# The order of VectorE's and GpSimd's work in the steps of a mixture-of-experts loop

## What is computed

```python
def routed_experts(xf, idx, wts, wg, wu, wd):
    ...
    padded = (counts + MOE_BLOCK - 1) // MOE_BLOCK * MOE_BLOCK
    ...
    def step(acc, inp):
        tok, w, e = inp
        xb = xf[tok]
        hid = jax.nn.silu(jnp.einsum('nrd,ndf->nrf', xb, wg[e].astype(F32))) * jnp.einsum('nrd,ndf->nrf', xb, wu[e].astype(F32))
        yb = jnp.einsum('nrf,nfd->nrd', hid, wd[e].astype(F32)) * w[..., None]
        acc = acc.at[tok.reshape(-1)].add(yb.reshape(-1, D_MODEL))
        return acc, None
```

## Time and profile before

| | us |
|---|---|
| median of three executions | 2057.08 |
| the profiled execution | 2054.86 |
| its span, first to last instruction | 2053.1 |
| TensorE busy in the span | 1992.9 (97%) |
| VectorE busy | 1134.7 (55%) |
| GpSimd busy | 781.3 (38%) |
| ScalarE busy | 505.2 (25%) |

### The profile page before, as it was taken

The page is one execution under the profiler, slowest core; times in us unless marked ns, Lnnn a source line. Parts: engine busy times, 40 slices in busy tenths (PEclk is TensorE's granted clock), DMA queues, the critical chain, the costliest instruction groups (busy, mean ns, idle before and its releaser), DMA issues.

```text
span 2053.1 us, 23779 instructions
## 1 busy us (share of the span) xinstructions
PE 1992.9 (97%) x7241; PEld 1005.4 (49%) x7242; DVE 1134.7 (55%) x3064; ACT 505.2 (25%) x1103; POOL 781.3 (38%) x717
## 2 busy tenths in 40 slices
PE   8999999999999999999999999999999999999994
PEld 6444667575544444444445554444444444444441
DVE  6221546776622222344776757966666666666645
ACT  3111554452312222224331221111111111111114
POOL 1762005622122221215990002654555545454531
PEclk9999999999999999999999999999999999999997
DMA  5421000011132222135257014999999999999964
GB/s 148 125 96 41 21 21 21 22 47 47 41 129 77 77 82 75 49 114 175 96 201 285 31 42 151 361 362 361 354 363 355 369 350 355 350 341 355 339 216 172
DMA packets 129639, 370.45 MB, mean 180 GB/s; under 512 B 33712, under 2 KB 65668, under 8 KB 103832
## 3 DMA queue, kind: packets, MB, share of 16 engines
q1 hardware_dynamic: 103960, 314.83, 41.3%
q0 software_dynamic: 23520, 54.61, 10.5%
q10 hardware_dynamic: 2080, 0.01, 0.1%
HBM read 320.57 MB, written 68.17 MB: 189 GB/s over the span
## 4 chain that ended last, share of the span: by engine, by line
PE 25%; DMA 20%; issue 4%; POOL 3%; DVE 3%; POOLq 0%; ACT 0%; SPq 0%; DVEq 0%
DMA sums<-arena,row_to 19%; PE banks L3219 9%; PE banks L2300 4%; PE banks L3235 4%; PE banks L2347 2%; POOL arena L2136 2%; PE banks L2014 2%; PE banks L279 1%; PE banks L2364 1%; PE banks L2323 1%; DVE arena L3212 1%; DVE index L3182 1%; DMA arena<-in_w_router_dram 0%; DVE arena L3337 0%; PE banks L3227 0%
## 5 line engine op out<-in xcount | busy, mean ns | idle before, releaser
L3219 PE MATMUL banks<-arena 128*128 128x512 f32 x1056 | 467.7, 596 | 3.9 <-issue 3.2
L3198 POOL DMA_INDIRECT arena<-h_rows,index x268 | 282.5, 1054 | 133.4 <-issue 78.8
L3219 PEld LDWEIGHTS banks<-arena 128*128 128x128 f32 x1056 | 197.4, 192 | 228.4 <-issue 228.4
L1720 PE MATMUL banks<-arena 128*128 128x512 f32 x672 | 299.0, 594 | 1.0 <-ACT arena L323 1.0
L3235 PE MATMUL banks<-arena 128*128 128x512 f32 x528 | 237.6, 593 | 1.3 <-ACT arena L3033 0.8
L3206 POOL DMA_INDIRECT sums<-arena,row_to x66 | 109.0, 1652 | 268.4 <-DMA sums<-arena,row_to 229.0
L279 PE MATMUL banks<-arena 128*128 128x512 f32 x416 | 192.1, 599 | 2.2 <-PEq L108 2.2
L1720 PEld LDWEIGHTS banks<-arena 128*128 128x128 f32 x672 | 123.1, 190 | 135.5 <-issue 133.9
L3212 DVE STREAM_TRANSPOSE arena<-arena 128x1024 f32<-128x1024 f32 x66 | 133.7, 2026 | 57.6 <-PE banks L3219 57.5
L3182 DVE TENSOR_SCALAR index<-row 32x1 uint32<-32x1 f32 x1072 | 155.2, 145 | 17.1
L3235 PEld LDWEIGHTS banks<-arena 128*128 128x128 f32 x528 | 100.1, 190 | 126.5 <-issue 124.8
(11 more groups left out here) (414 smaller groups left out, 2424.0 us busy)
## 6 DMA issues: line engine op xcount, KB each, us to landing
arena<-in_w_exp_gate_dram SPq DMA_DIRECT2D x66, 1024.0 KB, 7.1
arena<-in_w_exp_up_dram SPq DMA_DIRECT2D x66, 1024.0 KB, 10.6
arena<-in_w_exp_down_dram SPq DMA_DIRECT2D x66, 1024.0 KB, 16.4
arena<-in_w_in_dram SPq DMA_DIRECT2D x26, 1024.0 KB, 5.3
gates<-arena SPq DMA_DIRECT2D x60, 256.0 KB, 2.0
arena<-gates SPq DMA_DIRECT2D x15, 1024.0 KB, 7.6
arena<-h_rows,index POOLq DMA_INDIRECT x268
arena<-in_x_dram SPq DMA_DIRECT2D x8, 512.0 KB, 5.8
```

What stands on the lines that cost most here:

```text
L1720: mm = pe.matmul(gate_bank(n, b), left[:, k, :], right[:, k, :], start=(alone and k == 0), stop=(k == 3), skip_group_check=True)
L3198: return pool.indirect_dma_start(w.x[k][:, 256 * q:256 * (q + 1)], None, rows, bass.IndirectOffsetOnAxis(ap=g.index[:, k, q:q + 1], axis=0 ...
L3219: mm = pe.matmul(g.bank[:, 2, :].rearrange("p (a f) -> p a f", a=2), xT[:, k, :], wgu[:, :, k, :], start=(k == 0), stop=(k == KT - 1))
```

## The change

It moves work within a step and adds or removes no computation.

- VectorE's order in every step but step 0 is: take_rows(b-1), the reading of the list of b+3 (`take_list`), turned(b+1), select(b+4), hidden(b), result(b-1), and last the rest of index(b+3) (`make_index`). Of the two branches behind `if not has(i, c, -1)` the first is always taken.
- GpSimd issues scatter(b-1) first and gather(b+3) after it.
- `overflow_tables` has seven parts instead of four, done in steps 0 to 6. The four large operations are cut into halves of 24x64 elements a partition.
- `run` writes out steps 0 to 7; the hardware loop begins at step 8.

```diff
--- before.py
+++ after.py
@@ -2646,24 +2646,36 @@
 
     ovhot = g.region(TABLES, 48, NE)
     over, ovend, ones, iota48 = g.over, g.ovend, g.ones64, g.iota48
+    halves = slice(0, 24), slice(24, 48)
+
+    def reached(h):
+        then(dve.tensor_tensor(ovhot[:, h], bcast(iota48[:, h].unsqueeze(2), [P, 24, NE]),
+                               bcast(ovend.unsqueeze(1), [P, 24, NE]), ALU.is_ge))
+
+    def weighed(h):
+        then(dve.tensor_tensor(ovhot[:, h], ovhot[:, h], bcast(over.unsqueeze(1), [P, 24, NE]), ALU.mult))
+
     if part == 0:
         then(dve.tensor_tensor_scan(ovend, ones, over, 0.0, ALU.mult, ALU.add))
         then(dve.tensor_scalar(g.ovmore[:, 0:1], ovend[:, NE - 1:NE], -float(AHEAD), 1.0, ALU.add, ALU.max))
         then(dve.tensor_copy(g.ovn[:], g.ovmore[:, 0:1]))
-
-        then(dve.tensor_tensor(ovhot, bcast(iota48.unsqueeze(2), [P, 48, NE]),
-                               bcast(ovend.unsqueeze(1), [P, 48, NE]), ALU.is_ge))
+        reached(halves[0])
     if part == 1:
-        then(dve.tensor_reduce(g.ovef, ovhot, AX.X, ALU.add))
+        reached(halves[1])
+        then(dve.tensor_reduce(g.ovef[:, halves[0]], ovhot[:, halves[0]], AX.X, ALU.add))
+    if part == 2:
+        then(dve.tensor_reduce(g.ovef[:, halves[1]], ovhot[:, halves[1]], AX.X, ALU.add))
         then(dve.tensor_scalar(g.ovef, g.ovef, float(NE - 1), None, ALU.min))
         then(dve.tensor_copy(g.ovexp[:], g.ovef))
-    if part == 2:
-
+    if part == 3:
         then(dve.tensor_scalar(g.idle, ovhot[:, :, NE - 1], 2.0 * T, None, ALU.mult))
-        then(dve.tensor_tensor(ovhot, ovhot, bcast(over.unsqueeze(1), [P, 48, NE]), ALU.mult))
-    if part == 3:
-        then(dve.tensor_reduce(g.shift[:], ovhot, AX.X, ALU.add))
-
+        weighed(halves[0])
+    if part == 4:
+        weighed(halves[1])
+    if part == 5:
+        then(dve.tensor_reduce(g.shift[:, halves[0]], ovhot[:, halves[0]], AX.X, ALU.add))
+    if part == 6:
+        then(dve.tensor_reduce(g.shift[:, halves[1]], ovhot[:, halves[1]], AX.X, ALU.add))
         then(dve.tensor_tensor(g.shift[:], iota48, g.shift[:], ALU.subtract))
         then(dve.tensor_scalar(g.shift[:], g.shift[:], 1.0, float(P), ALU.add, ALU.mult))
         dve.tensor_tensor(g.shift[:], g.shift[:], g.idle, ALU.add).then_inc(tabled, 1)
@@ -2739,9 +2751,9 @@
     def run(eng, before, step, ready, after):
 
         before()
-        for c in range(4):
-            step(0, c)
-        with eng.Fori(1, NE // 4 - 1) as i:
+        for b in range(8):
+            step(*divmod(b, 4))
+        with eng.Fori(2, NE // 4 - 1) as i:
             for c in range(4):
                 step(i, c)
         ready()
@@ -2899,11 +2911,17 @@
                 else:
                     select_rows(g, dve, w, g.iota[:], b).then_inc(s["q"], 1)
 
-            def index(i, c):
+            def take_list(i, c):
                 dve.wait_ge(s["lst"], val(i, c) + 1)
                 if has(i, c, -4):
                     dve.wait_ge(s["to"], 2 * val(i, c) - 6)
                 list_rows(g, dve, w, c % 4).then_inc(s["list"], 1)
+
+            def index(i, c):
+                take_list(i, c)
+                make_index(i, c)
+
+            def make_index(i, c):
                 dve.wait_ge(s["list"], val(i, c) + 1)
                 index_flags(g, dve, w, c % 4).then_inc(s["flag"], 1)
                 dve.wait_ge(s["flag"], val(i, c) + 1)
@@ -2959,6 +2977,18 @@
                     hidden(i, c)
                     index(i, c + 3)
                     select(i, c + 4)
+                elif has(i, c, -1):
+                    take_rows(i, c - 1)
+                    if has(i, c, 3):
+                        take_list(i, c + 3)
+                    if has(i, c, 1):
+                        turned(i, c + 1)
+                    if has(i, c, 4):
+                        select(i, c + 4)
+                    hidden(i, c)
+                    result(i, c - 1)
+                    if has(i, c, 3):
+                        make_index(i, c + 3)
                 else:
                     take_rows(i, c - 1)
                     if has(i, c, 3):
@@ -2968,13 +2998,12 @@
                     if has(i, c, 1):
                         turned(i, c + 1)
                     hidden(i, c)
-                if has(i, c, -1):
                     result(i, c - 1)
-                else:
+                if not has(i, c, -1):
                     first.last_sum()
-                if isinstance(i, int) and i == 0:
                     dve.wait_ge(g.sums_begun, 64)
-                    overflow_tables(g, dve, c, then, s["tabled"])
+                if isinstance(i, int) and i < 2 and val(i, c) < 7:
+                    overflow_tables(g, dve, val(i, c), then, s["tabled"])
 
             def ready():
                 picked.extend(chosen_expert(dve, k) for k in range(AHEAD + 1))
@@ -3099,10 +3128,10 @@
                 first.gpsimd(pool, lambda b: gather(0, b))
 
             def step(i, c):
+                if has(i, c, -1):
+                    scatter(i, c - 1)
                 if has(i, c, 3):
                     gather(i, c + 3)
-                if has(i, c, -1):
-                    scatter(i, c - 1)
 
             def after():
                 pool.wait_ge(stored[0], 16 * (NE // 2))
```

## The result

The change costs 2%: 2100.64 us (median of four) against 2056.76 (2055.85 to 2059.7) on the same chip, a ratio of 1.0205, 95% interval 1.0193 to 1.0217. The profiled execution took 2099.67 us, its span 2097.8, that is 44.7 more than the span before. Lines of the changed kernel: up products L3248, lists L2830, turn of hidden L3256, down L3264; on VectorE turned L3241, select L3189, product of hidden L2946, result L2953; GpSimd's scatter L3235, gathers L3227.

A forecast was written before the change was run, and what follows sets the result against it. It took TensorE to bound the first half of the expert loop and the chain of scatters the second. Span 2053.1 less 1.7, plus 1.8 and 2.2 from span to median, gave 2055.4 us, range 2050 to 2067.

The forecast's parts named there:

- The lists of b+4 need select too, but select ends before H does, so that costs nothing more: TensorE's list products at the step's end: waiting for select adds nothing, as select ends before the product of hidden.
- The floor of 10.99: TensorE's step with select between turn and product of hidden: 10.99 us with the short restart, 11.36 at the loop boundary.
- The ring: Scatter, later gathers, turn, products and next scatter: 41.6 us for four steps, 10.4 a step, some 3 us in hand.
- L = 11.2: Length in us assumed for one link of the scatter chain, each scatter waiting for the last; 11.29 was the mean before.
- links over 11.5 fall where issues meet select: Scatter chain: reason given for taking 11.2 us a link, since select now has a fixed place away from the scatter.
- is covered: VectorE's index work behind the result: hidden in 4 us of idle time a step, ahead of the next turn.
- The start: Start of the expert loop: third expert's up products at 1291.1 instead of 1294.91, fourth scatter at 1327.9 instead of 1333.02.
- The end: Last experts: up products of the last at 1984.0, last scatter at 2014.4, 1.7 us less than before.
- Rival (b): Select on the path costs the long restart in every step, 11.36 us: 2069; chance 0.30 with long scatter links.
- Rival (a): Expert loop falls to TensorE's new floor, 10.99 us in every step, scatter links under 11.1: 2051; chance 0.27.
- rival (c): Full DMA engines decide, order does nothing in the loop, only the start counts: 2053 to 2060; 0.43 with the main forecast.
- The rule on the shared port: VectorE and GpSimd lock a port pair: select would hold each step's last gather 0.8 us, without changing the sum.

The follow-up runs named there:

- e9: Changed kernel with list products in the hardware loop reading expert 0's values at a fixed address and gathers ahead of the scatter again: 2063.21 us, ratio 1.0028.
- e1: Changed kernel with select ahead of the turn again, GpSimd's new order kept: 2075.06 us, ratio 1.0085.
- e3: Changed kernel with list products in the hardware loop reading expert 0's values at a fixed address: 2069.11 us, ratio 1.0056.
- e5: Kernel before with only GpSimd's order changed, scatter ahead of the gathers: 2074.89 us, ratio 1.0070.
- e13: Changed kernel with eight tiny products at the same register addresses ahead of TensorE's wait for select, in the hardware loop: 2070.33 us, ratio 1.0064.
- e6: Changed kernel with select ahead of the turn and gathers ahead of the scatter again, index work still last: 2063.11 us, ratio 1.0024.
- e7: Kernel before with only the tables in seven pieces and eight steps written out: 2058.34 us, ratio 1.0005.
- e14: Changed kernel with the eight tiny address-making products ahead of the wait and gathers ahead of the scatter again: 2064.53 us, ratio 1.0034.
- e2: Changed kernel with only GpSimd's order undone, gathers ahead of the scatter again: 2098.16 us, ratio 1.0199.

## Why the prediction was wrong

It said 2055.4 us, 2050 to 2067; 2100.64 was measured, 31.6 us above the slowest case that it priced (2069). By its own steps:

- **"The lists of b+4 need select too, but select ends before H does, so that costs nothing more"** is the step that failed, and it is worth 0.7 to 0.8 us in each of 51 steps, some 40 us. It took the duration of the lists, 0.34 us, from a place where their wait had long been met. I had looked at when the wait is met and not at what TensorE does between the wait and the products. In the trace of before nothing comes to register-addressed products through a wait, but the size stood there all the same: the eight address instructions of its list line start between 1530.1 and 1531.0, hidden under other products (the view of L2818 above). Behind the wait they alone take these 0.9 us, and the lists with them 1.05, for the 0.34 that the forecast took.
- **The floor of 10.99** was right: product of hidden at +10.20 for 10.21, written-out steps of 11.01, and a median of 11.01 for the steps of e9 that aren't at the loop boundary. At the boundary six of e9's twelve steps are 11.33 to 11.38, for a forecast 11.36; the others are longer, up to 12.25.
- **The ring** was mis-sized by less. In e1, where all turns wait for gathers, the turn starts 13.29 us after the first gather (12.68 to 14.35, steps 8 to 59; taken: 13.0) and 15.37 after S(b-1) (taken: 14.9). From up(b+4) to S(b+3) the trace of after has 12.6 us, where "10.3 + 0.75 + 0.7" = 11.75 were counted. With both, four steps need 15.4 + 3.9 + 11.1 + 12.6 = 43.0 us, 10.75 a step: nearer to the link of 11.2, with 1.8 us in hand and not 3. Both kinds of wait then share the steps, and e1, e3 and e5 run at 11.3 to 11.4 (e13 at 11.3 too, but there TensorE alone needs 11.25). "L = 11.2" was a size too good for this order: 11.3 in e3, 11.4 in e1 and e5. The sum doesn't explain that, with its 1.8 us in hand; what does stays open, as said under e5. The reason given for a link shorter than 11.29, "links over 11.5 fall where issues meet select", was a misreading: of the twelve links over 11.5 from S(3) to S(60) before, four hold a slow gather and one a slow scatter issue, and the other five slow gathers stand in links of 10.9 to 11.1.
- **The index work "is covered"** was wrong by a little: with the gathers behind the scatter it is (e5 has it early and is no faster than e1), with the gathers first it costs 0.2% (e6 against e7).
- **The start** was about right. In this execution up(0) is 2.75 us later than before; less that, up(2) is at 1291.2 (said: 1291.1), S(0) at 1294.2 (said: 1293.6) and S(3) at 1328.7 (said: 1327.9). Timeline of the changed kernel, which answers to the earlier trace rows:

```profile
1282.72 7.03 PE L3248 MATMUL banks<-arena 128*128 128x512 f32 x16
...
1293.91 6.60 PE L3248 MATMUL banks<-arena 128*128 128x512 f32 x15
...
1296.98 1.64 POOL L3235 DMA_INDIRECT sums<-arena,row_to  x1 [6.27 <-DMA sums<-arena]
```

- **The end**: the last scatter comes 31.1 us after up(64) (2060.47 - 2029.37) for a forecast 30.3. Steps 60 and 61, written out but with an expert number held in a register, show the same 1.05 us:

```profile
1994.78 1.06 PE L2830 MATMUL banks<-arena 128*128 x8 [0.42 <-DVE arena L3189]
...
2006.99 1.05 PE L2830 MATMUL banks<-arena 128*128 x8 [0.41 <-DVE arena L3189]
```

- **Rival (b)** gave the right sign with the wrong mechanism: not the long restart of up in every step (the boundary's), since with fixed addresses the same wait gives steps of 11.0. Its side remark, gathers that land too late (it named over 16 us, e1 has 13.3), points at a real cost of GpSimd's order, 0.3% once the addresses are out of the way (e13 to e14) and hidden in the changed kernel. **Rival (a)** and **rival (c)** are out: the pace is above the floor everywhere in the hardware loop, and the DMA share fell to 0.95 to 0.97.
- **The rule on the shared port** (the Trainium skill, page "SBUF — State Buffer", who interferes with whom) decided nothing: of 225 gathers from step 8 on, nine took over 1.15 us before, and none of 228 now. Select lies behind the last gather, not beside it. The trace of before shows the hold only one way: the nine slow gathers are those that began in the first 0.81 us of a select, and each ended 2.1 us after that select's start, while in 39 cases in which the gather began first select took its usual 1.22 to 1.23 us. Also the rule on turns of packets (the Trainium skill, page "DMA: Bandwidth & Descriptors") could not be tested by L, as L follows the step.

By a rule of the Trainium skill the failed step could have been met. Its page "Perfetto Trace Analysis", sections "Sequencer Loop" and "Per-engine timelines", says that an instruction for the engine is pushed to a queue, where it waits for its semaphores while the sequencer goes on, but a control instruction waits in the sequencer itself. The runs agree: with the wait on the first product (fixed address) the lists take 0.35 us, with the wait on an address instruction 1.05, with the addresses ahead of the wait 0.35 again. In the timeline views the address instructions don't appear; the view of the line shows them, 0.9 us of them behind select's end in the changed kernel.

## What to carry to other kernels

Before an instruction is moved so that its reader comes to it through a wait, look at what the reader's engine must still do between the wait and the work: here addresses held in registers were free under other products and cost their full time behind a wait. The trace of the kernel before has their number and their spacing, in the view of the line and not in the timeline. If they can't be avoided, they can be made ahead of the wait, as eight tiny products with the same addresses did here for 0.2 us a step. And when two orders are changed at once, test each on the kernel before: here one hid the cost of the other completely (e2 moved nothing, e5 lost 0.7%).

## What was not expected of the hardware

- Eight products of 128x6 whose addresses come from registers take 1.05 us when they follow a wait and 0.34 us when the wait was met earlier; the address instructions ahead of them start 0.12 us apart (median, both kernels). Eight further products at addresses already made cost 0.22 us.
- Adding eight products to a step shortened it from 11.89 to 11.31 us.
- The time lost to addresses stands in the profile as busy time of the products (50.0 us for 375 against 17.5 for 408), not as idle time ahead of them.
